# Routing weights of the second expert layer: one-hot matmuls replaced by accumulating indirect DMAs into a cleared matrix

## The chip, the cores and the metric

The kernel runs on one core of one Trainium2 chip. The metric is the device time of one launch in microseconds (us), the median of the timed runs. All arithmetic is float32; a matrix product is done as three products of a high and a low part.

## The reference, cut to what matters

The program is a two-layer block (attention and convolution, an expert layer; a recurrent mLSTM mixer, a second expert layer) followed by a second two-layer transformer. The change is in the second expert layer, and a part of it lies in the mLSTM stage before. An expert layer does this for each token `t` (256 tokens in the second layer, D = 1024, 8 heads, 128 keys per side, so 16384 experts, 16 chosen per head):

```
q = (xb @ w_q).reshape(PEER_BLOCK, PEER_HEADS, 2, PEER_DHALF)
s = jnp.einsum('thpd,hpkd->thpk', q, subkeys).astype(jnp.float32)
s1, i1 = lax.top_k(s[:, :, 0], PEER_TOPK)
s2, i2 = lax.top_k(s[:, :, 1], PEER_TOPK)
cand = s1[..., :, None] + s2[..., None, :]          # 16 x 16 pairs
cidx = i1[..., :, None] * PEER_NKEYS + i2[..., None, :]
top, pos = lax.top_k(cand, PEER_TOPK)
idx = jnp.take_along_axis(cidx, pos, axis=-1)
g = jax.nn.softmax(top, axis=-1)
act = jax.nn.gelu(jnp.einsum('td,thkd->thk', xb, u[idx]))
return jnp.einsum('thk,thkd->td', g * act, v[idx])
```

## The kernel before

The kernel does not gather the chosen experts of the second layer. It computes all 16384 activations for all 256 tokens, multiplies them by a routing matrix that is zero where an expert was not chosen, and multiplies the result by all of v. The expert number is i * 128 + j, with i the first and j the second index of the pair; the routing matrix has one value for each j, i and token.

The function is `experts` (line 964). All engines walk the same slots. The up phase has 144 slots: in each, a piece of 128 x 1024 weights (16 pieces of w_q, 128 of u, one for each j) is loaded by SP into `w_raw` (ring of 3), split into a high part by ScalarE (line 168) and a low part by VectorE (line 173), and multiplied by TensorE in 24 matmuls of 256 columns (`project`). The result of a u piece goes through Gelu on ScalarE and is stored to memory (`spilled`, line 1136). The down phase has 128 slots over v: SP loads the piece and reads the stored activations of 128 experts again (line 1156), VectorE multiplies them by the routing values (`weigh`, line 1535), they are split, and TensorE adds 12 products of 512 columns to four banks (`combine`).

The queries come in four passes of two heads. In the slots after a pass VectorE ranks its scores (`rank_step`, 15 steps spread over 18 slots) and leaves the indices i and j in `sel[:, t, 0]` and `sel[:, t, 1]`. After the last pass only, `centre` (slot 78), an Exp on ScalarE (slot 79) and `normalise` (slot 80) make the softmax weights of all heads, in `sel[:, t, 2]`. Then `turn` (slot 81) transposes the three lists, so that the picks of a token lie along the partitions, and for 64 groups of four tokens (`route`, slots 84 to 135) VectorE and ScalarE build a one-hot matrix of i and one of j that carries the weights, TensorE multiplies them (line 1225: 4 matmuls of 128 x 128, 8 records in the trace), ScalarE copies the result (line 1311), and SP stores it in chunks of 16 tokens of 1 MB (line 1140). When all chunks are stored (waits at line 1144) SP reads the matrix back, 8 values of j at a time (line 1149), into a ring of two.

The order within an engine is the order of the slots in its loop: SP's loads, stores and reads of all these kinds stand in one queue. In the second layer POOL has only the root of the norm. In the first layer, which shares this function, POOL also issues 256 indirect gathers of expert rows for one tile of tokens (line 1167). That layer keeps its way of routing.

The stage before the second expert layer is `mlstm` (line 1808). It loads 33 weight pieces of 512 KB on SP through a ring of three (`Pieces.sp_load`, line 1781), which waits for the split of the piece three before.

Of the kernel before, what the change touches and what calls it, by code (L numbers as in the profile page):

```python
# [17 lines left out]
P = 128  # L18
# [945 lines left out]
def experts(nc, ident, consts, w_q, subkeys, u, v, xs, tiles, gate_rows, spans, spilled, routed_dram, sparse_from):  # L964
# [13 lines left out]
    u_rows, gathered = sparse_from or (None, ())  # L978
    GATHERED = NT - 1 if sparse_from else None
# [6 lines left out]
    pairs_done = {1: 0, 3: 1} if NT > TT else {3: 0}  # L986
# [15 lines left out]
    NG = N // 4  # L1002
# [25 lines left out]
    NC = N // GT  # L1028
    chunk_last = [route_at[4 * k + 3] for k in range(NC)]
    read_from = chunk_last[-1] + (6 if GATHERED is not None else 3)  # L1030

    with Stage(nc) as st:
# [31 lines left out]
        G = arena.at(0, "routing_chunk", [P, 2, NC, JC, GT])  # L1064
# [12 lines left out]
        else:  # L1077
# [21 lines left out]
             "routing_staged", "weighed_ready", "weighed_high_ready", "weighed_split", "sum_kept"))  # L1099
        block = st.begin()  # L1100
# [14 lines left out]

        def bank(n, t):
            return (side if n == 0 else hidden)[:, t, :] if NT == 4 else side[:, 2 * n + t, :]

        @block.sync
        def _(sp):  # L1120
# [3 lines left out]
            sp.dma_start(keys[:, :, :], subkeys).then_inc(keys_loaded, 16)  # L1124
            for s in range(-AHEAD, SLOTS):
# [19 lines left out]
                for k in range(PE_K // JC):  # L1145
                    if s == (read_from + k if k < 2 else UP + JC * (k - 1) - 1):
                        if k >= 2:
                            sp.wait_ge(weighed_ready, JC * (k - 1))
                        sp.dma_start(G[:, k % 2], routed_dram[:, :, k * JC * GT:(k + 1) * JC * GT]
# [9 lines left out]
        def _(pool):  # L1159
            normed.pool_root(pool)  # L1160
            for n, (kind, k) in enumerate(items):
                if n == 0:
                    pool.wait_ge(chosen, 1)
                if n >= GR:
# [4 lines left out]
                    .then_inc(gathered[n % GR], 16)  # L1169

        @block.tensor
        def _(pe):
# [56 lines left out]
            def combine(d):  # L1229
                s = UP + d  # L1230
                pe.wait_ge(weighed_split, d + 1)
                for n in range(2):
                    pe.wait_ge(split, 2 * s + n + 1)
                    if d == 0:
                        pe.wait_ge(staged_in, NG)
                        pe.wait_ge(evacuated, UP)
# [8 lines left out]
            for s in range(UP):  # L1245
# [4 lines left out]
                if s == turn_at:  # L1250
                    turn()
# [7 lines left out]
        def _(act):  # L1259
# [79 lines left out]
            for s in range(SLOTS):  # L1339
# [6 lines left out]
                if s - 1 in finish:  # L1346
                    act.wait_ge(centred, finish[s - 1] + 1)
                    pair = tiles_of(finish[s - 1])
                    nc.scalar.activation(ex[:, pair], top[:, pair].rearrange("p t (h k) -> p t h k", k=K), ACT.Exp) \
                        .then_inc(exp_done, 1)  # L1350
# [4 lines left out]
                if s == turn_at + 1:  # L1355
                    keep_picks()
# [13 lines left out]
        def _(dve):  # L1370
# [96 lines left out]
            def centre(event):  # L1467
                pair = tiles_of(event)
                chain.settle()
                chain.wrote(nc.vector.tensor_copy(total[:, pair], tops[:, pair, :, 0]))  # L1470
                chain.settle()
                nc.vector.tensor_tensor(tops[:, pair], tops[:, pair],
                                        total[:, pair].unsqueeze(3).broadcast_to([P, TT, H, K]), ALU.subtract) \
                    .then_inc(centred, 1)

            def normalise(event):
                pair = tiles_of(event)
                dve.wait_ge(exp_done, event + 1)
                chain.wrote(nc.vector.tensor_reduce(total[:, pair], ex[:, pair], X, ALU.add))
                chain.settle()  # L1480
                chain.wrote(nc.vector.reciprocal(total[:, pair], total[:, pair]))
                chain.settle()
                for t in range(pair.start, pair.stop):
                    last = nc.vector.tensor_tensor(sel[:, t, 2, :].rearrange("p (h k) -> p h k", h=H), ex[:, t],
                                                   total[:, t].unsqueeze(2).broadcast_to([P, H, K]), ALU.mult)
# [42 lines left out]
            def weigh(d):  # L1528
# [4 lines left out]
                if d >= 2:  # L1533
                    dve.wait_ge(weighed_split, d - 1)
                nc.vector.tensor_tensor(weighed[:, d % 2, :].rearrange("p (c t) -> p c t", t=GT),  # L1535
# [272 lines left out]
def mlstm(nc, ident, consts, cols, norm, gate_row, w, xs):  # L1808
# [21 lines left out]
    with Stage(nc) as st:  # L1830
# [31 lines left out]
        half = st.sbuf("minus_half", [P, 2])  # L1862
        acc = [st.psum(f"acc{r}", [P, 512]) for r in range(4)]
# [22 lines left out]
        def _(sp):  # L1886
# [14 lines left out]
        def _(pool):  # L1901
            normed.pool_root(pool)
# [1467 lines left out]
```

## Time and profile before

| | us |
|---|---|
| median of three timed runs | 4600.79 (4597.6 to 4608.13) |
| profiled execution | 4594.13 |
| its span, first to last instruction | 4592.4 |
| TensorE matmul busy | 4179.2 (91%) |
| VectorE busy | 3223.5 (70%) |
| ScalarE busy | 2216.7 (48%) |
| POOL busy | 322.4 (7%) |

The mean granted TensorE clock of the profiled execution was 0.955 of full speed. All other times below are counted from the start of its span. The mLSTM stage runs from 1842 to 2056 us, the second expert layer from 2060 to 2945. Busy time of TensorE is modelled from pipelined matmuls: consecutive records overlap, so a duration of 0.28 us does not mean that a matmul costs 0.28 us; the distance of two starts does. PE is TensorE, PEld its weight load, DVE VectorE, ACT ScalarE, POOL GpSimd, SP the queue engine.

### The profile page before, as it was taken

Reading aid. Unit: us, or ns where it says so; the run is one execution under the profiler, and the core shown is the slowest. Engines: PE = TensorE matmul, PEld = TensorE weight load, DVE = VectorE, ACT = ScalarE, POOL = GpSimd, SP = SyncE. Lnnn points to the kernel's source line nnn. Section 1 sums busy time; section 2 is a strip of 40 time slices with the busy share of each in tenths; the row PEclk is TensorE's granted clock in tenths of the full one; section 3 lists DMA queues with packets and bytes.
Section 4 is the critical chain, followed back from the end, with each engine's and each line's share of the span. In section 5 each row is a group of like instructions: output and inputs, shape, how many; then the busy total and the mean of one; then the engine's idle time right before and its main releaser. Section 6 shows DMA issues by size and latency. Waiting matters only on the chain. (4 is left out here: it accounts for less than half of the span.)

```text
span 4592.4 us, 70641 instructions
## 1 busy us (share of the span) xinstructions
PE 4179.2 (91%) x25113; PEld 3660.3 (80%) x25113; DVE 3223.5 (70%) x7301; ACT 2216.7 (48%) x4317; POOL 322.4 (7%) x301
## 2 busy tenths in 40 slices
PE   7869899999999999889999999699888999988898
PEld 2445799999977777669999777598876889887687
DVE  7636599999878787558877576665486556548655
ACT  6514344367633333335478455444355444435543
POOL 0000002422322221000000000000000000000000
PEclk9889899999999999899999999899999999999899
DMA  8611358888999997227777888554444445444343
GB/s 303 214 40 37 97 166 281 292 277 307 341 360 341 339 335 256 87 88 213 213 232 248 267 261 262 173 185 155 131 134 137 174 165 185 158 126 130 132 176 140
DMA packets 398128, 936.24 MB, mean 204 GB/s; under 512 B 35736, under 2 KB 210072, under 8 KB 381188
## 3 DMA queue, kind: packets, MB, share of 16 engines
q1 hardware_dynamic: 360968, 798.21, 52.4%
q0 software_dynamic: 36864, 134.23, 8.4%
q8 instruction: 167, 2.74, 0.2%
q14 instruction: 129, 1.06, 0.1%
HBM read 838.89 MB, written 93.42 MB: 203 GB/s over the span
## 5 line engine op out<-in xcount | busy, mean ns | idle before, releaser
L173 DVE TENSOR_TENSOR w_low__7<-w_raw__2,w_high__7 128x512 fp32r<-128x512 f32 x544 | 362.3, 688 | 119.6 <-ACT w_high__7 L168 104.8
L173 DVE TENSOR_TENSOR w_low__6<-w_raw,w_high__6 128x512 fp32r<-128x512 f32 x576 | 381.3, 686 | 68.8 <-ACT w_high__6 L168 66.1
L161 PE MATMUL hidden<-hT_high__2,w_high__6 128*128 128x384 f32 (+1 forms) x1280 | 423.5, 331 | 6.5 <-DVE w_low__6 L173 6.5
L162 PE MATMUL hidden<-hT_low__2,w_high__6 128*128 128x384 f32 (+1 forms) x1280 | 419.5, 328 | 0.0
L163 PE MATMUL hidden<-hT_high__2,w_low__6 128*128 128x384 f32 (+1 forms) x1280 | 419.0, 327 | 0.0
L168 ACT ACTIVATE w_high__6<-w_raw 128x512 fp32r<-128x512 f32 x576 | 339.9, 625 | 160.0 <-PE side L163 66.7
L168 ACT ACTIVATE w_high__7<-w_raw__2 128x512 fp32r<-128x512 f32 x544 | 322.0, 624 | 71.3 <-PE side__2 L163 35.7
L161 PE MATMUL hidden__3<-hT_high__4,w_high__7 128*128 128x256 f32 x1152 | 333.4, 289 | 0.0
L162 PE MATMUL hidden__3<-hT_low__4,w_high__7 128*128 128x256 f32 x1152 | 328.7, 285 | 0.0
L163 PE MATMUL hidden__3<-hT_high__4,w_low__7 128*128 128x256 f32 x1152 | 328.2, 285 | 0.0
L161 PEld LDWEIGHTS hidden<-hT_high__2,w_high__6 128*128 128x128 f32 x1280 | 242.3, 189 | 7.8 <-issue 7.2
L163 PEld LDWEIGHTS hidden<-hT_high__2,w_low__6 128*128 128x128 f32 x1280 | 242.5, 189 | 0.0
L162 PEld LDWEIGHTS hidden<-hT_low__2,w_high__6 128*128 128x128 f32 x1280 | 242.3, 189 | 0.0
L161 PE MATMUL side__2<-w_high__7,weighed_high__2_23558 128*128 128x512 f32 x512 | 205.7, 402 | 23.4 <-DVE weighed_low__2_23559 L173 15.3
L161 PEld LDWEIGHTS hidden__3<-hT_high__4,w_high__7 128*128 128x128 f32 x1152 | 220.4, 191 | 0.0
L162 PEld LDWEIGHTS hidden__3<-hT_low__4,w_high__7 128*128 128x128 f32 x1152 | 220.1, 191 | 0.0
L163 PEld LDWEIGHTS hidden__3<-hT_high__4,w_low__7 128*128 128x128 f32 x1152 | 220.1, 191 | 0.0
L162 PE MATMUL side__2<-w_low__7,weighed_high__2_23558 128*128 128x512 f32 x512 | 203.5, 397 | 0.0
L163 PE MATMUL side__2<-w_high__7,weighed_low__2_23559 128*128 128x512 f32 x512 | 203.4, 397 | 0.0
L1167 POOL DMA_INDIRECT gathered_rows<-in_peer_v,chosen_experts x128 | 163.9, 1281 | 418.2 <-DVE gathered_sum L1512 374.8
L168 ACT ACTIVATE weighed_high<-weighed 128x384 fp32r<-128x384 f32 x128 | 67.2, 525 | 247.7 <-DVE weighed L1535 160.7
L1167 POOL DMA_INDIRECT gathered_rows<-in_u_rows,chosen_experts x128 | 140.4, 1097 | 569.8 <-DVE dots L1499 344.8
(980 smaller groups left out, 12523.1 us busy)
## 6 DMA issues: line engine op xcount, KB each, us to landing
w_raw<-in_peer_u SPq DMA_DIRECT2D x128, 512.0 KB
w_raw<-in_peer_v SPq DMA_DIRECT2D x128, 512.0 KB
w_raw__2<-in_peer_u SPq DMA_DIRECT2D x128, 512.0 KB, 4.3
w_raw__2<-in_peer_v SPq DMA_DIRECT2D x128, 512.0 KB, 4.9
w_ring<-in_w_mod SPq DMA_DIRECT2D x96, 256.0 KB, 4.3
w_ring__2<-in_w_mod SPq DMA_DIRECT2D x96, 256.0 KB, 4.4
activated_dram<-activated SPq DMA_DIRECT2D x128, 192.0 KB
routing_dram<-routing SPq DMA_DIRECT2D x24, 1024.0 KB, 10.0
```

What stands on the lines that cost most here:

```text
L161: nc.tensor.matmul(out, lhs[0], rhs[0], start=start, stop=False, skip_group_check=True)
L162: nc.tensor.matmul(out, lhs[0], rhs[1], start=False, stop=False, skip_group_check=True)
L163: return nc.tensor.matmul(out, lhs[1], rhs[0], start=False, stop=stop, skip_group_check=True)
L168: return nc.scalar.activation(high, src, ACT.Copy)
L173: return nc.vector.tensor_tensor(low, src, high.bitcast(F32), ALU.subtract)
L1167: pool.indirect_dma_start(ring[:, n % GR, :], None, rows, bass.IndirectOffsetOnAxis(ap=chosen_at[:, k:k + 1], axis=0)) \
```

## The change

The routing matrix of the second layer gets the layout [j, i, token] in memory. It is set to zero in the mLSTM stage, by 32 DMAs of 512 KB from a tile of zeros that POOL fills; SP issues two of them after each of the piece loads 3 to 18, and waits for all of them at the end of its queue. In the expert layer `centre`, the Exp and `normalise` are done after each of the four passes, for its two heads. `normalise` also computes the address of each pick, (j * 128 + i) * 256 + token, and for each of the 16 picks of a head and each of the two tiles POOL issues an indirect DMA that adds 128 values of 4 bytes (one per token) to the matrix: 256 DMAs in all. A head's DMAs wait for those of the head before it in the same tile. SP waits for all of them in slot 140 and then reads the matrix, 8 values of j at a time, in contiguous runs of 256 tokens. The transposes of the picks, the one-hots, their matmuls, the evacuations and the stores of the routing chunks are gone in this layer. The arithmetic of the first layer is unchanged; its small instructions are issued per tile.

```diff
+    SCATTER = GATHERED is None
-    pairs_done = {1: 0, 3: 1} if NT > TT else {3: 0}
+    pairs_done = {1: 0, 3: 1} if NT > TT else {p: p for p in range(4)}
-    NG = N // 4
+    NG = 0 if SCATTER else N // 4
-    read_from = chunk_last[-1] + (6 if GATHERED is not None else 3)
+    read_from = UP - 4 if SCATTER else chunk_last[-1] + 6
...
 @@ SP
+                        if SCATTER:
+                            if k == 0:
+                                for t in range(NT):
+                                    for r in range(2):
+                                        sp.wait_ge(scattered[t][r], 16 * K * H // 2)
+                            sp.dma_start(G[:, k % 2], routed_dram[k * JC:(k + 1) * JC].rearrange("j i t -> i j t")) \
+                                .then_inc(G_loaded[k % 2], 16)
+                            continue
...
 @@ POOL
+            for p in range(4 if SCATTER else 0):
+                pool.wait_ge(selected, p + 1)
+                for h in range(p * HP, (p + 1) * HP):
+                    for t in range(NT):
+                        if h >= 1:
+                            pool.wait_ge(scattered[t][(h - 1) % 2], 16 * K * ((h - 1) // 2 + 1))
+                        for k in range(h * K, (h + 1) * K):
+                            pool.indirect_dma_start(routed_dram.rearrange("j i t -> (j i t)").unsqueeze(1),
+                                                    bass.IndirectOffsetOnAxis(ap=cell_at[:, t, k:k + 1], axis=0),
+                                                    sel[:, t, 2, k:k + 1], None, compute_op=ALU.add) \
+                                .then_inc(scattered[t][h % 2], 16)
...
 @@ VectorE, normalise
+                if SCATTER:
+                    part = slice(some.start * K, some.stop * K)
+                    dve.wait_ge(token_loaded, 16)
+                    for t in range(NT):
+                        last = nc.vector.scalar_tensor_tensor(flat_at[:, t, part], sel[:, t, 1, part], float(PE_K),
+                                                              sel[:, t, 0, part], ALU.mult, ALU.add)
+                    chain.wrote(last)
+                    chain.settle()
+                    for t in range(NT):
+                        last = nc.vector.tensor_scalar(cell_at[:, t, part], flat_at[:, t, part], float(N),
+                                                       token[:, t:t + 1], ALU.mult, ALU.add)
+                    chain.wrote(last)
...
 @@ mlstm, SP and POOL
+            sp.wait_ge(zeroed, 1)
             for n in range(3, len(sources)):
                 pieces.sp_load(sp, n)
+                if n < 3 + PE_K // 8:
+                    for j in (8 * (n - 3), 8 * (n - 3) + 4):
+                        sp.dma_start(cleared[j:j + 4].rearrange("j i t -> i j t"),
+                                     zeros[:, :].rearrange("p (j t) -> p j t", t=T)).then_inc(cleared_rows, 16)
+            sp.wait_ge(cleared_rows, 16 * PE_K // 4)
...
+            nc.gpsimd.memset(zeros[:, :], 0.0).then_inc(zeroed, 1)
```

## Rows read from the trace of the kernel before

**Rows 1.** Busy time by stretch: us, each engine's busy (records), clock, DMA share, GB/s.

```profile
2086.00:2320.00 234.00, 234.00 (x1958) 234.00 (x1957) 200.91 (x654) 121.67 (x253) 0.00 (x0) 1.00 0.76 215
2320.00:2530.00 210.00, 210.00 (x1791) 210.00 (x1790) 163.62 (x427) 173.26 (x352) 0.00 (x0) 1.00 0.76 244
2565.00:2935.00 370.00, 354.73 (x1499) 282.93 (x1498) 260.51 (x498) 192.13 (x372) 0.00 (x0) 0.99 0.84 258
```

**Rows 2.** Waits in the second expert layer: us, times, longest, for TensorE and SP.

```profile
PE side__2 L161 <- DVE weighed_low__2_23559 L173: 15.3, 14, 3.0
...
SPq L1144 <- DMA routing_dram<-routing__2_23555: 7.1, 1, 7.1
```

**Rows 3.** Timeline of TensorE, first matmul of the down phase: start, us, idle before.

```profile
2560.96 0.76 PE L161 MATMUL side__2<-w_high__7,weighed_high__2_23558 128*128 128x512 f32 x1 [8.10 <-ACT activated__2 L1278]
```

**Rows 4.** Timeline of TensorE around one routing group, up phase.

```profile
2441.44 1.05 PE L1225 MATMUL side__2<-weight_at_j__2_23553,one_hot_i__2_23552 128*128 128x128 f32 x8
...
2442.45 0.29 PE L162 MATMUL hidden__3<-hT_low__4,w_high__7 128*128 128x256 f32 x1
2442.57 0.28 PE L163 MATMUL hidden__3<-hT_high__4,w_low__7 128*128 128x256 f32 x1
...
2445.20 1.05 PE L1225 MATMUL side__2<-weight_at_j__2_23553,one_hot_i__2_23552 128*128 128x128 f32 x8
```

**Rows 5.** Groups by line, second expert layer: count, busy us, mean ns, idle before.

```profile
L173 DVE TENSOR_TENSOR w_low__7<-w_raw__2,w_high__7 128x512 fp32r<-128x512 f32 x544 | 362.3, 688 | 119.6 <-ACT w_high__7 L168 104.8
...
L1225 PE MATMUL side__2<-weight_at_j__2_23553,one_hot_i__2_23552 128*128 128x128 f32 x512 | 65.5, 275 | 0.0
```

**Rows 6.** DMA issues: count, KB each, median us from issue to landing.

```profile
routing_chunk__2_23556<-routing_dram SPq DMA_DIRECT2D x16, 1024.0 KB, 8.0
...
piece_raw<-in_qk SPq DMA_DIRECT2D x8, 512.0 KB, 3.6
```

**Rows 7.** Timeline of VectorE: centring and normalising, slots 78 and 80.

```profile
2307.79 0.42 DVE L1472 TENSOR_TENSOR top__2<-top__2,total__2 128x256 f32<-128x256 f32 x1
...
2314.93 0.41 DVE L1479 TENSOR_REDUCE total__2<-ex__2 128x16 f32<-128x256 f32 x1
...
2315.67 0.49 DVE L1484 TENSOR_TENSOR selected__3<-ex__2,total__2 128x128 f32<-128x128 f32 x2
```

**Rows 8.** Timeline of ScalarE, slot 79.

```profile
2308.72 1.28 ACT L1349 ACT_TABLE_LOAD   x1
```

**Rows 9.** Timelines of SP and POOL in the mLSTM stage.

```profile
1847.14 1.04 POOL L208 TENSOR_TENSOR inv__4<-mean__4,root__4 128x4 f32<-128x4 f32 x1 [0.47 <-DVE mean__4 L214]
...
1860.63 28.65 SPq L1781 DMA_DIRECT2D piece_raw<-in_qk  x6
1891.55 38.66 SPq L1781 DMA_DIRECT2D piece_raw<-in_v  x8
```

**Rows 10.** Busy time by stretch: mLSTM stage, and first expert layer.

```profile
1892.00:1932.00 40.00, 40.00 (x172) 32.96 (x171) 9.24 (x14) 10.72 (x19) 0.00 (x0) 0.96 0.34 98
...
1300.00:1500.00 200.00, 195.81 (x850) 158.79 (x849) 164.78 (x266) 78.71 (x146) 47.90 (x48) 1.00 0.98 343
```

**Rows 11.** Timeline of POOL, first gathers of the first expert layer.

```profile
719.66 1.32 POOL L1167 DMA_INDIRECT gathered_rows<-in_u_rows,chosen_experts  x1 [216.45 <-DVE chosen_experts L1489]
...
722.88 0.94 POOL L1167 DMA_INDIRECT gathered_rows<-in_u_rows,chosen_experts  x1 [0.30 <-issue]
...
728.45 0.94 POOL L1167 DMA_INDIRECT gathered_rows<-in_u_rows,chosen_experts  x1 [0.30 <-issue]
```

**Rows 12.** The gathers by tile: duration ns min/median/max, first and last start.

```profile
L1167 POOL DMA_INDIRECT gathered_rows<-in_u_rows,chosen_experts x128: 932/1008/1743, 719.7 to 1722.8; - x128
...
L1167 POOL DMA_INDIRECT gathered_rows<-in_peer_v,chosen_experts x128: 932/1007/2886, 770.5 to 1794.5; - x128
```

**Rows 13.** DMA queues: packets, MB, share of 16 engines' span.

```profile
q1 hardware_dynamic: 360968, 798.21, 52.4%
q0 software_dynamic: 36864, 134.23, 8.4%
```

More of the change, by code:

```diff
@@ L977, in experts @@
     NT = len(tiles)
-    u_rows, gathered = sparse_from or (None, ())
-    GATHERED = NT - 1 if sparse_from else None
+    u_rows, gathered = sparse_from
+    GATHERED = NT - 1 if u_rows is not None else None
     ND = NT if GATHERED is None else NT - 1
@@ L1099, in experts @@
              "routing_staged", "weighed_ready", "weighed_high_ready", "weighed_split", "sum_kept"))
+        token_loaded = st.sem("token_numbers_loaded")
+        scattered = [gathered[2 * t:2 * t + 2] for t in range(NT)]
         block = st.begin()
@@ L1249, in _ @@
                         score(p)
-                if s == turn_at:
+                if s == turn_at and not SCATTER:
                     turn()
@@ L1347, in _ @@
                     act.wait_ge(centred, finish[s - 1] + 1)
-                    pair = tiles_of(finish[s - 1])
-                    nc.scalar.activation(ex[:, pair], top[:, pair].rearrange("p t (h k) -> p t h k", k=K), ACT.Exp) \
-                        .then_inc(exp_done, 1)
+                    pair, some = tiles_of(finish[s - 1]), heads_of(finish[s - 1])
+                    for t in range(pair.start, pair.stop):
+                        last = nc.scalar.activation(ex[:, t, some], top[:, t].rearrange("p (h k) -> p h k", k=K)[:, some],
+                                                    ACT.Exp)
+                    last.then_inc(exp_done, 1)
                 if s in gelu_at:
@@ L1354, in _ @@
                     nc.scalar.activation(gelled[:, batch], dots[:, batch], ACT.Gelu).then_inc(gelu_done, 1)
-                if s == turn_at + 1:
+                if s == turn_at + 1 and not SCATTER:
                     keep_picks()
@@ L1482, in normalise @@
                 chain.settle()
                 for t in range(pair.start, pair.stop):
-                    last = nc.vector.tensor_tensor(sel[:, t, 2, :].rearrange("p (h k) -> p h k", h=H), ex[:, t],
-                                                   total[:, t].unsqueeze(2).broadcast_to([P, H, K]), ALU.mult)
+                    last = nc.vector.tensor_copy(total[:, t, some], tops[:, t, some, 0])
+                chain.wrote(last)
+                chain.settle()
+                for t in range(pair.start, pair.stop):
+                    last = nc.vector.tensor_tensor(
+                        tops[:, t, some], tops[:, t, some],
+                        total[:, t, some].unsqueeze(2).broadcast_to([P, some.stop - some.start, K]), ALU.subtract)
@@ L3226, in build @@
         first["gathered"] = [ctx.enter_context(nc.semaphore(f"rows_gathered{r}")) for r in range(GATHER_RING)]
+        first["scattered"] = [ctx.enter_context(nc.semaphore(f"weights_scattered{r}")) for r in range(2 * TT)]
         first_block(nc, ident, consts, cols, first, xs, mod_rows, spilled, routed)
```

68 lines of the change are left out of this document (45 added, 23 removed).

## The prediction

> **What bounds the kernel now.** I read the page first (TensorE busy for 91% of the span), then the table of busy time by stretch, the groups of instructions, the timelines of single engines, and the waits. The changed code is the second expert layer. It consists of an up phase (144 slots: 16 query pieces, 128 pieces of u) and a down phase (128 slots over v). In [rows 1] the reader is to see that TensorE is busy for every one of the 234 us before the routing and of the 210 us with it, at clock 1.00, while VectorE has 33 and 46 us to spare and ScalarE more. So there what TensorE issues sets the time, and work taken from VectorE or ScalarE alone buys nothing. In the down phase TensorE is busy 355 of 370 us, and its only wait of size is the one for the low part of the weighed activations, 15.3 us in 14 times [rows 2]. Between the phases it stands still for 8.10 us [rows 3].
>
> **What goes.** A plain up slot is 24 matmuls, which start 0.12 us apart (2442.45, 2442.57): 2.88 us. From one routing group's start to the next (2441.44 to 2445.20) it is 3.76 us [rows 4]. A group costs TensorE 0.88 us, there are 64, one in each of 52 slots or a second in a slot: 64 x 0.88 = 56.3 us. The six transposes of the picks go too; at the spacing of the eight records of one group (512 records in 64 [rows 5]: 0.88 / 8 = 0.11 us) they are 0.7 us. Together 57.0 us, all on the path, as TensorE never waits there. The one-hots on VectorE and the 64 evacuations on ScalarE go as well and count nothing: both engines lie beside TensorE. Next late in the freed stretch is TensorE itself at 2.88 us a slot: VectorE needs two splits of 0.69 us for it [rows 5].
>
> **The end of the up phase.** SP waits 7.1 us at line 1144 until the last stored routing chunks have landed, with the loads of v behind it [rows 2]; TensorE's 8.10 us follow from this [rows 3]. The changed kernel stores no chunks, and if the scatters are through by slot 140 the wait is nothing. Left is the read of the first chunk, 8.0 us [rows 6], issued three slots (8.6 us) before its use. I leave 2 us of the gap and count 6 us gained (bounds: 0 and 8.1).
>
> **The down phase.** A chunk of 1 MB was read in runs of 16 tokens by 8 j, 512 bytes; now they are 1 KB. The 14 waits for the low part (15.3 us in all [rows 2]) are one for each chunk read from k = 2 on. The bounds are 0 and 15.3; half the runs might halve the DMA's surplus, not the bytes, and I take a third, 5 us. The multiply of 128x256 keeps its size.
>
> **What is added on VectorE and ScalarE.** Centring and normalising now come after each of the four passes, over two heads and two tiles. The present ones take 0.42 us for the subtraction, 0.41 for the sum, 0.25 for each multiply [rows 7]. Fourteen small instructions a pass, at 0.17 to 0.29 us, are some 3.5 us; three passes more are 10 us out of 33 idle [rows 1]. The low part for slot s + 3 is made in slot s, so a pass may be late by two slots (5.8 us) before TensorE sees it. ScalarE gets three more Exp, each with two table loads of 1.28 us [rows 8], out of 112 us idle. I count 0.5 us for both, with the token load (bounds 0 and 5); without this cover it would be 10 + 8 us.
>
> **The clearing, in the recurrent stage before.** 32 DMAs of 512 KB follow piece loads 3 to 18 on SP's queue. SP first waits for POOL's fill of the zeros: POOL is through with its root at 1848.2, and SP's fourth load leaves only at 1860.63 [rows 9], so 12 us cover the fill. Pieces leave every (38.66 - 0.33) / 7 = 5.48 us. Three times the bytes in that time is 1.57 MB / 5.48 us = 287 GB/s; the stretch had 98 GB/s [rows 10]. Traffic with many 1 KB runs has moved at 258 GB/s at share 0.84 [rows 1], and long rows at 343 [rows 10]. At 343 it fits; at 258 each piece is 0.6 us late, 16 pieces 10 us, against a load that lands in 3.6 us [rows 6] and is wanted two pieces (11 us) later. Bounds 0 and 20 us (the upper one if writes in 1 KB runs go slower than any row shows); I take 2, since the two rows near 287 fall either side.
>
> **The scatters.** 256 indirect DMAs of 128 elements on POOL, each adding 4 bytes. Nothing else is on POOL in the stage, but SP waits for all of them at slot 140, and behind it in SP's queue stand the first two routing chunks, the loads of v from slot 147 on, the last stored activations and the first ones read again: TensorE needs all of these. So the date of the last scatter decides this change.
> - Start: the weights were done at 2316.2 [rows 7], in slot 80. The first pass is now done in slot 26, 54 slots earlier: 54 x 2.88 = 155.5, and three blocks of scores of 16 such records as in the routing, 3 x 16 x 0.11 = 5.3. That gives 2155.4.
> - Date: TensorE ended the up phase at 2560.96 - 8.10 = 2552.9 [rows 3], now 57.0 earlier: 2495.9. Less a chunk's landing (8.0) and a scatter's landing (no row; I take a piece's 3.6 [rows 6]): the last one must leave at 2484.3.
> - 328.9 us for 256: the allowance is 1.285 us each. Passes come 54 us apart and bring 64 each, 82 us of work, so POOL doesn't run dry.
> - Price: the trace has indirect gathers of 128 rows of 4 KB, none that scatters or adds. Their instruction is 0.93 us at least, 1.01 in the median, with 0.30 between two: 1.24 or 1.31 [rows 11, 12]. Seven back to back, beside a full VectorE, leave every (728.45 - 719.66) / 6 = 1.465 us [rows 11]. Below: 1.24. Above: an accumulation may want twice the work of writing it down, 2 x 1.01 + 0.30 = 2.3 us. I take 1.31, the median: one entry for each of 128 partitions is what a scatter has too, and VectorE is less full here than beside those seven. 256 x 1.31 = 335.4, so SP and TensorE are late by 6.5 us.
> - The waits of head h for head h - 1 of the same tile stand 16 issues (21 us) behind: nothing.
>
> **Sum.** -57.0 - 6 + 6.5 - 5 + 0.5 + 2 = -59.0 us. The profiled execution took 4594.13 us (span 4592.4 and 1.7 around it); that gives 4535.1. The median of the timed runs, 4600.79, lies 6.7 above it, so I forecast 4542 for such a median. Its own range, with intervals of 1.24 to 1.45 and the bounds above, is 4522 to 4580. Every 0.01 us on a scatter's interval beyond 1.285 costs 2.6 us; the gain without stall is 65.5 us, so the change breaks even at 1.285 + 65.5 / 256 = 1.54 us.
>
> **Rivals.**
> - **A. An adding scatter costs POOL more than a gather (ends slower).** Each element is read at its source and at its target and then written: three accesses to write down for two. With the 1.01 us growing by half, the interval is 1.01 x 1.5 + 0.30 = 1.81; the last leaves at 2155.4 + 463.4 = 2618.8, 134.5 us late instead of 6.5: 4594.1 - 65.5 + 134.5 = 4663 in the profiled execution, 4670 as a median. It decides from 1.54 us on. For it: the shortest gather was 932 ns with either source [rows 12], and POOL went on before the rows had landed, so the time goes into writing the transfer down, not into moving it. Against: a fixed part of it may be large. Chance 0.24. On its premise the Trainium skill, "DMA: Bandwidth & Descriptors", section "Rules for kernel authors", says that an accumulating DMA reads its destination and writes it later; no row here shows what this costs.
> - **B. The DMA engines can't take the small packets (ends slower).** SP's queue moves 640 KB per 2.88 us, 228 GB/s of the 350 that 343 at share 0.98 means [rows 10]: 65%. A gather made 36864 / 256 = 144 packets, 9 an engine; scatters would be 2304 an engine. At the mean of SP's queue, 0.524 x 4592.4 x 16 / 360968 = 107 ns [rows 13], they are 246 us; with 214 of the rest this is 460 us of work in 329: +131 us, so 4594 - 65.5 + 131 = 4660, 4666 as a median. At 50 ns they just fit. The 107 ns are for 2.2 KB, which speaks against it; that each adds in memory speaks for it. Chance 0.12.
> - **C. VectorE holds POOL up.** The first gather, which began beside VectorE's splits, took 1.32 us, the third 0.94 [rows 11]. Splits fill 2 x 0.69 of 2.88 us, less their overlap some 42%: 0.94 + 0.42 x 0.38 + 0.30 = 1.40 us. 256 x 1.40 = 358.4: 29.5 us late, 23 above the forecast: 4565 as a median. Chance 0.14. The Trainium skill, "SBUF — State Buffer", section "Who interferes with whom", has this as a rule: a VectorE instruction with two inputs in SBUF contends with a GpSimd instruction that reads SBUF; the trace agrees by the 1.32 against 0.94 us.
> - **D. The clearing starves the piece loads**: 20 us instead of 2, 4559. Chance 0.04.
> - **E. The gain is eaten to nothing**: an interval of 1.50 to 1.58. 4590 to 4611. Chance 0.05.
>
> **Chances and range.** Forecast 0.41, C 0.14, D 0.04: 0.59, all faster. A and B 0.36, slower, though the mildest of A may be near the break-even. E 0.05. A measurement here can tell 0.2% (9 us) from no change. Faster 0.60, same 0.04, slower 0.36. Both signs hold much chance, so the range must reach over A and B: 4522 to 4675; above it is POOL's upper bound of 2.3 us (+125 us more than A).
>
> **What would show it.** In the changed profile: no matmul at line 1225 in the second layer and up slots of 2.88 us to the end (if they are longer and ScalarE waits for loads of w_raw, B); 256 DMA_INDIRECT on POOL from about 2155 on, whose interval is 1.31 (C: 1.40 with long ones beside splits; A: 1.5 or more throughout); SP's wait for scattered at slot 140 as the one before the first matmul of the down phase, under 8 us by the forecast, over 100 by A; pieces 5.5 us apart in the recurrent stage. The forecast is wrong if that last wait is above 30 us.

## The result, and the profile after

| | before | after |
|---|---|---|
| median of the timed runs, us | 4599.19 (4 runs) | 4708.93 (4 runs) |
| profiled execution's span, us | 4592.4 | 4694.2 |
| up phase, first matmul to end, us | 481.3 | 418.2 |
| gap before the down phase, us | 8.1 | 179.4 |
| down phase, first to last matmul, us | 379.8 | 373.5 |

The kernel got slower: ratio 1.0232, 95% interval 1.0210 to 1.0254. The forecast was 4542, with 0.6 on faster. The time is rival A's case and beyond it: 4709 where A gave 4670.

The page of the changed kernel first: TensorE's busy time, the two large DMA queues, and the new group of instructions (busy us, mean ns, idle before).

```profile
PE 4115.7 (88%) x24595; PEld 3593.7 (77%) x24595; DVE 3134.8 (67%) x7039; ACT 2128.0 (45%) x4137; POOL 747.8 (16%) x558
...
q1 hardware_dynamic: 359320, 798.22, 51.2%
q0 software_dynamic: 73728, 134.38, 10.0%
...
L1199 POOL DMA_INDIRECT routing_dram<-selected__3,routing_cells x256 | 423.1, 1653 | 172.8 <-DVE selected__3 L1539 95.0
```

TensorE is busy for 63.5 us less than before, as meant, and the time is longer all the same: busy time that goes is not time won. The table by stretch shows where it went. Its stretches are the up phase, the gap and the down phase; they answer to [rows 1].

```profile
2077.00:2495.00 418.00, 418.00 (x3522) 418.00 (x3520) 293.57 (x843) 225.15 (x461) 280.86 (x164) 0.99 0.89 222
2495.00:2674.60 179.60, 0.27 (x3) 0.06 (x1) 1.71 (x4) 1.31 (x4) 142.27 (x93) 0.51 0.25 13
2674.60:3049.00 374.40, 364.98 (x1536) 290.44 (x1536) 264.91 (x507) 194.31 (x377) 0.00 (x0) 0.99 0.81 261
```

The reader is to see the middle row. For 180 us every engine but POOL stands still, and the DMA engines are at share 0.25. POOL is the only one at work, and the 142 us that it is busy in 180 are one instruction after another with 0.3 us between them. The waits say for whom (these answer to [rows 2]; us, times, longest):

```profile
PE side__2 L161 <- ACT activated__2 L1311: 179.4, 1, 179.4
PE side__2 L161 <- DVE weighed_low__2_23605 L173: 9.2, 10, 2.0
...
SPq L1167 <- DMA routing_dram<-selected__3,routing_cells: 179.8, 2, 150.3
```

The first row names ScalarE's last activation, which had long been done: it is the last semaphore in the list of the waiting matmul. The third row has the true one: SP at line 1167 waits for the scatters, with the first chunks and the loads of v behind it. The scatters began like this (timeline of POOL):

```profile
2164.43 1.83 POOL L1199 DMA_INDIRECT routing_dram<-selected__3,routing_cells  x1 [95.00 <-DVE selected__3 L1539]
2166.56 1.56 POOL L1199 DMA_INDIRECT routing_dram<-selected__3,routing_cells  x1 [0.30 <-issue]
2168.42 1.55 POOL L1199 DMA_INDIRECT routing_dram<-selected__3,routing_cells  x1 [0.30 <-issue]
2170.28 6.22 POOL L1199 DMA_INDIRECT routing_dram<-selected__3,routing_cells  x1 [0.31 <-issue]
2176.80 1.61 POOL L1199 DMA_INDIRECT routing_dram<-selected__3,routing_cells  x1 [0.30 <-issue]
```

The last one left at 2663.79, so the interval is 499.36 / 255 = 1.958 us, where I had 1.31 and a break-even of 1.54. Nothing in the price is waiting for an earlier one: the idle time between two is "issue", 0.30 us, throughout. Three instructions took over 6 us. That is what VectorE did in the same time as the first of them:

```profile
2170.13 2.48 DVE L173 TENSOR_TENSOR w_low__7<-w_raw__2,w_high__7 128x512 fp32r<-128x512 f32 x4
2172.53 0.22 DVE L1458 CAST where_f__2<-where__2 128x128 bf16<-128x128 uint32 x1
2172.66 1.22 DVE L1459 TENSOR_TENSOR pair_scores__2_23594<-best__2 128x1024 f32<-128x1024 f32 x1
2173.80 1.29 DVE L173 TENSOR_TENSOR w_low__7<-w_raw__2,w_high__7 128x512 fp32r<-128x512 f32 x2
2175.01 0.42 DVE L1423 MAX8 head_top__2<-pair_scores__2_23594 128x8 f32<-128x256 f32 x1
```

The long scatter starts inside an unbroken run of subtractions, cast and addition, and ends at 2176.50, which is 1.49 us after the start of the MAX8 that closes the run.

### The profile page after: what moved, and what is told of

Read it like the earlier page. It is cut to its first block and busy times, and to the rows that moved or that the text cites. A ratio compares the mean times of both kernels' runs of the same rounds, so it can differ in the third digit from the quotient of the medians.

```text
span 4694.2 us, 69369 instructions
## 1 busy us (share of the span) xinstructions
PE 4115.7 (88%) x24595; PEld 3593.7 (77%) x24595; DVE 3134.8 (67%) x7039; ACT 2128.0 (45%) x4137; POOL 747.8 (16%) x558
## 5 line engine op out<-in xcount | busy, mean ns | idle before, releaser
L1199 POOL DMA_INDIRECT routing_dram<-selected__3,routing_cells x256 | 423.1, 1653 | 172.8 <-DVE selected__3 L1539 95.0
L162 PE MATMUL hidden<-hT_low__2,w_high__6 128*128 128x384 f32 (+1 forms) x1280 | 418.4, 327 | 0.0
L161 PE MATMUL side__2<-w_high__7,weighed_high__2_23604 128*128 128x512 f32 x512 | 205.3, 401 | 188.7 <-ACT activated__2 L1311 179.4
L161 PE MATMUL hidden__3<-hT_high__4,w_high__7 128*128 128x256 f32 x1152 | 324.7, 282 | 0.0
L162 PE MATMUL hidden__3<-hT_low__4,w_high__7 128*128 128x256 f32 x1152 | 324.2, 281 | 0.0
L163 PE MATMUL hidden__3<-hT_high__4,w_low__7 128*128 128x256 f32 x1152 | 324.2, 281 | 0.0
L161 PEld LDWEIGHTS side__2<-w_high__7,weighed_high__2_23604 128*128 128x128 f32 x512 | 97.2, 190 | 217.3 <-DVE weighed_low__2_23605 L173 195.0
L161 PEld LDWEIGHTS hidden__3<-hT_high__4,w_high__7 128*128 128x128 f32 x1152 | 218.2, 189 | 0.0
L162 PEld LDWEIGHTS hidden__3<-hT_low__4,w_high__7 128*128 128x128 f32 x1152 | 218.1, 189 | 0.0
L163 PEld LDWEIGHTS hidden__3<-hT_high__4,w_low__7 128*128 128x128 f32 x1152 | 218.1, 189 | 0.0
L1592 DVE TENSOR_TENSOR weighed__2_23603<-activated_again__2_23606,routing_chunk__2_23602 128x256 f32<-128x256 f32 x128 | 53.9, 421 | 234.7 <-DMA activated_again__2_23606<-activated_dram 234.1
```

Of the source, the lines that this page charges most:

```text
L161: nc.tensor.matmul(out, lhs[0], rhs[0], start=start, stop=False, skip_group_check=True)
L162: nc.tensor.matmul(out, lhs[0], rhs[1], start=False, stop=False, skip_group_check=True)
L163: return nc.tensor.matmul(out, lhs[1], rhs[0], start=False, stop=stop, skip_group_check=True)
L1199: pool.indirect_dma_start(routed_dram.rearrange("j i t -> (j i t)").unsqueeze(1), bass.IndirectOffsetOnAxis(ap=cell_at[:, t, k:k + 1], axi ...
L1592: nc.vector.tensor_tensor(weighed[:, d % 2, :], act_in[:, d % AD, :], G[:, k % 2, d % JC, :], ALU.mult) \
```

## The experiments

The recurrent stage began at 1846.6 and 1860.2 us in the two profiles of the code of before, and between 1845.2 and 1856.7 us in the eight of the changed code, whose first layer differs only in how small instructions are issued. So single times are read to about 10 us, and the stages of the second layer are compared by their own lengths.

### Is it the adding, the scatter, or the number of cells?

Plain writes in place of adding ones (e1_plain):

```diff
-                                sel[:, t, 2, k:k + 1], None, compute_op=ALU.add)
+                                sel[:, t, 2, k:k + 1], None)
```

> The scatters write instead of adding (left out: the sum where two heads of a token chose the same expert). Everything else as in the changed kernel. Theory 1, the adding is what makes a scatter dear on POOL: the instruction falls from 1.54 us (median) to the 0.93 to 1.01 us of the gathers of the first layer, the interval from 1.96 to about 1.31 us, the last scatter of 256 issues near 2164 + 335 = 2499, and the gap of TensorE before the down phase falls from 179 us to about 20; time about 4709 - 160 = 4550. Theory 2, it is scattering itself, adding or not: instruction 1.54 us, interval 1.96 us, gap 179 us, time 4709. Theory 3, adding costs at the DMA engines alone (a read and a write at each cell) and POOL is held back by them: the landing, 2.9 us in the changed kernel, falls, and the interval with it, but not to 1.31.

The same cells gathered into a buffer (e3_gather4):

```diff
-    pool.indirect_dma_start(cells_of(routed_dram), IndirectOffsetOnAxis(ap=cell_at[:, t, k:k + 1], axis=0),
-                            sel[:, t, 2, k:k + 1], None, compute_op=ALU.add)
+    pool.indirect_dma_start(fetched[:, t, k:k + 1], None, cells_of(routed_dram),
+                            IndirectOffsetOnAxis(ap=cell_at[:, t, k:k + 1], axis=0))
```

> Each of the 256 scatters is turned round into a gather of the same 128 cells of 4 bytes, from the routing matrix into a column of a buffer in SBUF (left out: the routing weights never reach the matrix). Theory 1, direction decides (an instruction that scatters costs 1.54 us, one that gathers 0.93 to 1.01, whatever its size): interval about 1.31 us, gap about 20 us, time about 4550. Theory 2, the form of the list decides (128 separate cells of 4 bytes, in place of 128 rows of 4 KB): 1.54 us, interval 1.96 us, gap near 179 us, time 4709.

Adding scatters over 64 partitions (e4_64):

```diff
-    IndirectOffsetOnAxis(ap=cell_at[:, t, k:k + 1], axis=0), sel[:, t, 2, k:k + 1], None, compute_op=ALU.add
+    IndirectOffsetOnAxis(ap=cell_at[0:64, t, k:k + 1], axis=0), sel[0:64, t, 2, k:k + 1], None, compute_op=ALU.add
```

> Each of the 256 adding scatters takes partitions 0 to 63 alone, 64 cells in place of 128 (left out: the weights of the other half of the tokens). Theory 1, POOL pays for each cell: of 1.54 us half goes, interval 1.96 - 0.77 = about 1.2 us, the last scatter issues before 2484, gap below 10 us, time about 4535. Theory 2, POOL pays for the instruction: interval stays between 1.8 and 1.96 us, gap 140 to 179 us, time 4670 to 4709. In between, the two intervals at 64 and 128 cells give a fixed part and a part for each cell.

Measured, one run each: 4578.21, 4577.65 and 4689.22 us. TensorE's gap before the down phase is 50.0, 46.6 and 161.4 us, the interval of the instructions 1.456, 1.442 and 1.890 us. The instruction by tile (duration ns min/median/max, first and last start us), for the plain scatter:

```profile
L1199 POOL DMA_INDIRECT routing_dram<-selected__3,routing_cells x256: 954/959/5405, 2165.7 to 2537.0; - x128
```

for the gather:

```profile
L1200 POOL DMA_INDIRECT fetched_cells<-routing_dram,routing_cells x256: 940/946/5432, 2171.1 to 2538.9; - x128
```

and for the adding scatter over 64 partitions:

```profile
L1199 POOL DMA_INDIRECT routing_dram<-selected__3,routing_cells x256: 1421/1427/4949, 2172.9 to 2654.8; - x128
```

A plain scatter costs POOL 0.96 us and a gather of the same cells 0.95, close to the 0.93 of the shortest gather of 4 KB rows [rows 12]: neither direction nor size matters much to it. Adding makes it 1.54: 0.58 us more. Half the cells save 0.12 of 1.54 us, some 1.8 ns a cell: of the 1.54 us about 0.23 go with the number of cells and 1.31 are fixed. A plain scatter of 64 cells was not run, so at least 0.35 of the adding's 0.58 us are a price for the instruction, and how the rest divides is not shown. Of the first two, theory 1 was right about the instruction; of the third, theory 2. Theory 3 of the plain scatters (POOL held back by the DMA engines) does not fit: in both kernels POOL idles 0.30 us between two, and what shrank is the instruction itself. From the last scatter's start to the first down matmul it is 10.9 us with adding and 10.0 without.

But theory 1's time for the first two, 4550, was missed by 28 us, and that is a second finding. Their interval is not 1.31 us, though the median instruction is shorter than the 1.01 that I had assumed. The plain kernel's timeline of POOL shows why, once beside VectorE's subtractions and once in the gap, when VectorE had stopped (e1_plain):

```profile
2398.56 1.28 POOL L1199 DMA_INDIRECT routing_dram<-selected__3,routing_cells  x1 [0.30 <-issue]
2400.14 0.96 POOL L1199 DMA_INDIRECT routing_dram<-selected__3,routing_cells  x1 [0.30 <-issue]
2401.41 1.28 POOL L1199 DMA_INDIRECT routing_dram<-selected__3,routing_cells  x1 [0.30 <-issue]
2402.99 0.96 POOL L1199 DMA_INDIRECT routing_dram<-selected__3,routing_cells  x1 [0.30 <-issue]
...
2535.76 0.96 POOL L1199 DMA_INDIRECT routing_dram<-selected__3,routing_cells  x1 [0.30 <-issue]
2537.03 0.96 POOL L1199 DMA_INDIRECT routing_dram<-selected__3,routing_cells  x1 [0.30 <-issue]
```

And VectorE in the same kernel and time:

```profile
2401.16 1.29 DVE L173 TENSOR_TENSOR w_low__7<-w_raw__2,w_high__7 128x512 fp32r<-128x512 f32 x2 [1.56 <-ACT w_high__7 L168]
2404.01 1.29 DVE L173 TENSOR_TENSOR w_low__7<-w_raw__2,w_high__7 128x512 fp32r<-128x512 f32 x2 [1.55 <-ACT w_high__7 L168]
```

Here a scatter that starts inside a pair of subtractions is 0.32 us longer; the ones between pairs, and all of them after VectorE has stopped, take 0.96. Over 256 the mean is 1.150 against a shortest of 0.954: VectorE costs 0.196 us a scatter, 50 us in all. Counted over the whole kernel, 110 of the 256 start beside a subtraction or an addition of the pair scores, and they hold 46.9 of these 50 us. In the changed kernel it is 66 of 256, which hold 26.3 of 28.2 us above 1.542 us each. Even without adding, the scatters come too late: the gap of this kernel is 50.0 us.

### Does VectorE hold the scatter?

Two breaks in VectorE's run (e8_break):

```diff
                 elif k == 5:
+                    nc.vector.max(breaks[:, p, 0, :], iota)
                     nc.vector.tensor_copy(where_f[:, :, :, :], where[:, :, :, :])
-                    chain.wrote(nc.vector.tensor_tensor(cand[...], best[...], best[...], ALU.add))
+                    nc.vector.tensor_tensor(cand[...], best[...], best[...], ALU.add)
+                    chain.wrote(nc.vector.max(breaks[:, p, 1, :], iota))
```

> The changed kernel with two MAX8 of a constant row (0.3 us each, results unused) put into VectorE's step that makes the pair scores: one ahead of the cast to bf16, one behind the addition. In the changed kernel three scatters took 6.2 to 6.3 us, each from the start of an unbroken run of VectorE's subtractions, cast and addition until the MAX8 behind it began, plus 1.54. Theory 1, such a run holds POOL's scatter off and MAX8 lets it through: the first MAX8 comes 2.5 us after the run's start, so the three long ones shrink to 3.9 to 4.2 us. Theory 2, they are something periodic of POOL's own or of its queue: they stay at 6.2 to 6.3 us. The span changes by less than 10 us either way.

Measured: 4711.54 us (one run). Timeline of POOL beside the second of the three runs:

```profile
2229.89 3.86 POOL L1200 DMA_INDIRECT routing_dram<-selected__3,routing_cells  x1 [0.30 <-issue]
2234.06 2.56 POOL L1200 DMA_INDIRECT routing_dram<-selected__3,routing_cells  x1 [0.30 <-issue]
```

Timeline of VectorE there:

```profile
2229.86 2.48 DVE L173 TENSOR_TENSOR w_low__7<-w_raw__2,w_high__7 128x512 fp32r<-128x512 f32 x4
2232.26 0.28 DVE L1459 MAX8 breaks__2<-iota 128x8 f32<-128x128 f32 x1
...
2233.93 1.27 DVE L173 TENSOR_TENSOR w_low__7<-w_raw__2,w_high__7 128x512 fp32r<-128x512 f32 x2
2235.13 0.42 DVE L1424 MAX8 head_top__2<-pair_scores__2_23602 128x8 f32<-128x256 f32 x1
```

The 6.3 us are 3.86 now (3.74 and 3.86 at the other two): the scatter is through 1.49 us after the MAX8 that was put in. The next one starts in the following pair of subtractions, and again ends 1.49 us after the start of the MAX8 behind that pair (2236.62 and 2235.13). Theory 1 held. TENSOR_TENSOR alone does this, as the run of four shows; MAX8 lets the scatter through. This agrees with the Trainium skill, "SBUF — State Buffer", section "Who interferes with whom", by which a VectorE instruction with two SBUF inputs blocks a GpSimd one that reads SBUF. The same section infers that writing down a transfer is not hit by tensor_tensor; for an indirect DMA the 3.86 against 1.54 us say otherwise.

But the hold does not always last to the end of a run. In the plain kernel's pair above, the second subtraction started at 2401.77, and the scatter was through 0.91 us later, at 2402.69: it got in between the two. In the changed kernel, of 48 scatters that start inside the first of such a pair, 36 end 1.50 us after the start of the second subtraction and only 5 follow the whole pair. What decides between the two is not shown.

### Do the other terms of the sum hold?

Only the scatters of heads 0 to 3, so that nothing is late (e2_half):

```diff
-            for p in range(4 if SCATTER else 0):
+            for p in range(2 if SCATTER else 0):
...
-                                        sp.wait_ge(scattered[t][r], 16 * K * H // 2)
+                                        sp.wait_ge(scattered[t][r], 16 * K * H // 4)
```

> Only the 128 scatters of heads 0 to 3 are issued (left out: the routing weights of heads 4 to 7); the clearing, the additions on VectorE and ScalarE and the reads of the chunks stay. Theory 1, the whole loss is the wait for the last scatter, and the other terms of my sum hold: the first down matmul no longer waits (gap 1 to 3 us, of 179.4), the up phase stays at 418 us, the down phase at 374 us, time 4709 - 177 = 4532 us, ratio to the kernel before 0.985. Rival, the scatters also slow what runs beside them (VectorE held off SBUF, DMA engines busy with small packets): with half of them gone the up phase becomes shorter than 418 us by 3 us or more and a down phase without queued scatters too, time below 4528. Rival, once the wait is gone another one takes its place before the first chunk read or the first weighed block (a landing of 7.8 us behind the last up piece): gap of 8 us or more, time above 4538.

Measured in 3 rounds: 4537.71 us (4525.20 to 4540.92), ratio 0.9862, interval 0.9846 to 0.9879. Its up and down phases by stretch:

```profile
2071.00:2489.00 418.00, 417.78 (x3517) 417.61 (x3516) 293.34 (x842) 225.37 (x460) 228.20 (x128) 1.00 0.88 226
2491.00:2880.00 389.00, 365.30 (x1534) 291.13 (x1535) 264.67 (x506) 194.65 (x378) 0.00 (x0) 0.99 0.78 251
```

TensorE's waits in the down phase:

```profile
PE side__2 L161 <- DVE weighed_low__2_23605 L173: 23.5, 14, 3.0
PE side__2 L161 <- ACT activated__2 L1311: 1.4, 1, 1.4
```

The gap is 1.4 us and the up phase the same 418 us (418.4) with half as many scatters beside it, so the scatters take nothing from TensorE. Theory 1 held for the time. The down phase did not: 388.6 us, 9 longer than before. Over the ten profiles of this document:

| kernel | gap, us | down phase, us | its waits for the low part, us |
|---|---|---|---|
| before | 8.1 | 379.8 | 15.3 |
| before, buffers moved (below) | 8.7 | 386.1 | 18.2 |
| half the scatters | 1.4 | 388.6 | 23.5 |
| clearing twice (below) | 0.6 | 383.0 | 19.6 |
| one tile of two (below) | 3.2 | 386.6 | 21.0 |
| gather | 46.6 | 383.4 | 18.5 |
| plain | 50.0 | 380.5 | 14.5 |
| 64 partitions | 161.4 | 378.1 | 14.5 |
| two breaks | 177.0 | 379.8 | 15.6 |
| changed kernel | 179.4 | 373.5 | 9.2 |

The difference of the last two columns is 363 to 368 us each time: the waits, not the matmuls, make the length, and 1 KB runs in place of 512 bytes are not shown to lower them. The two kernels with the routing of before lie 6.3 us apart, and the one with the breaks has the changed kernel's pause and the length of before:

```profile
L161 PE MATMUL side__2<-w_high__7,weighed_high__2_23612 x512: 390/393/767, 2679.1 to 3058.9; 128*128 128x512 f32 x171
```

So the 6.3 us that the changed kernel gained here are no more than the spread between profiles. Pauses of 46 us and more go with somewhat shorter down phases, but the two groups overlap, and no run tried a pause by itself.

The clearing done twice, on top of this kernel (e7_clear2):

```diff
                         sp.dma_start(cleared[j:j + 4]..., zeros...).then_inc(cleared_rows, 16)
+                        sp.dma_start(cleared_too[j:j + 4]..., zeros...).then_inc(cleared_rows, 16)
```

> As the kernel with the scatters of heads 0 to 3 alone, and the clearing done twice (a second matrix of 16.8 MB is cleared beside the first and not used). Theory 1, the clearing is hidden (it cost 1.1 us of the mLSTM stage in the changed kernel): from the mLSTM stage's start to the first up matmul 226 to 229 us, and no other stage moves. Theory 2, the loads of the pieces were near their limit and the second 16.8 MB starve them: 16.8 MB at the 343 GB/s that the trace of before shows elsewhere are 49 us beside 33 MB of pieces in the same 36 us, so the stage grows by 30 us or more.

Measured: 4542.24 us (one run). From the stage's start (fill of its root) to the first up matmul it is 225.0 us before (225.2 with moved buffers), 226.2 after, 225.6 with half the scatters and 236.8 here: the second 16.8 MB cost 11 us, the first about 1.1 (0.5 to 2.6 over the kernels that clear the whole matrix once). Neither theory had the 11 us. Busy time in the stretch of the clearing in the changed kernel (last two columns: DMA share and GB/s; before they were 0.34 and 98 [rows 10]):

```profile
1892.00:1932.00 40.00, 37.51 (x174) 31.08 (x174) 12.66 (x22) 11.31 (x21) 0.00 (x0) 1.00 0.98 320
```

and with the clearing done twice:

```profile
1905.00:1985.00 80.00, 68.48 (x289) 55.35 (x288) 20.41 (x50) 20.41 (x44) 3.06 (x8) 0.94 1.06 363
```

One clearing fills the DMA engines to 0.98 and just fits; the next one is late.

### What the up phase gained beyond 57 us

The up phase fell by 62.9 us (first to last matmul 480.7 to 417.8), not 57. Its matmuls came every 0.119 us in place of 0.120. The kernel before, with nothing changed but three unused buffers set aside in the second expert layer (e6_moved):

```diff
+        if sparse_from is None:
+            st.sbuf("flat_experts", [P, NT, H * K])
+            st.sbuf("routing_cells", [P, NT, H * K], U32)
+            st.sbuf("token_numbers", [P, TT])
```

> The kernel before with three small unused buffers (2 x 1 KB and 8 bytes in each partition) set aside where the changed kernel has its cell numbers, so that all later buffers of the second expert layer lie at the changed kernel's places. Theory 1, the up phase's matmuls of 256 columns come every 0.119 us in place of 0.120 in the changed kernel because their buffers lie elsewhere: here too the median matmul is 281 to 282 ns (287 before) and the up phase is 3 to 5 us shorter than 481 us. Theory 2, it has to do with what was taken out (one-hots) or the shape of the program: 287 ns and 481 us stay.

The high x high matmuls of the up phase by tile, in the kernel before (duration ns min/median/max, first and last start):

```profile
L161 PE MATMUL hidden__3<-hT_high__4,w_high__7 x1152: 274/287/562, 2071.6 to 2552.3; 128*128 128x256 f32 x192
```

and in this one:

```profile
L161 PE MATMUL hidden__3<-hT_high__4,w_high__7 x1152: 277/280/562, 2085.4 to 2559.7; 128*128 128x256 f32 x192
```

474.3 us in place of 480.7: 6.4 us come from where the buffers lie, and 62.9 - 6.4 = 56.5 are the routing's, against 57.0 forecast. That is from one profile each; the up phases of the six other kernels without one-hots are 418.4 to 420.1 us, so 54 to 56.5 is what can be said. Theory 1 held, if a little stronger than expected. Its time, 4606.81 us, is one run and shows no gain: in the same profile the down phase is 6.3 us longer than before. Which address does it stays open.

### A version that beats both

The adding scatters are worth having as far as they fit before slot 140. So the first tile of 128 tokens is scattered (128 instructions) and the second keeps its one-hots (32 groups); the cleared matrix is half as large (e5_hybrid). This version computes everything.

```diff
-    NG = 0 if SCATTER else N // 4
+    HOT = (1,) if SCATTER else tuple(range(ND))
+    NG = len(HOT) * P // 4
...
+            G0 = arena.at(0, "routing_cells_chunk", [P, 2, JC, P])
+            G = arena.at(8 * KB, "routing_chunk", [P, 2, NC, JC, GT])
...
-                    for t in range(NT):
+                    for t in range(1):
                         if h >= 1:
                             pool.wait_ge(scattered[t][(h - 1) % 2], 16 * K * ((h - 1) // 2 + 1))
...
+                    nc.vector.tensor_tensor(weighed[:, d % 2, 0:P], act_in[:, d % AD, 0:P], G0[:, k % 2, d % JC, :], ALU.mult)
```

> A version that computes everything: the first tile of 128 tokens gets its routing weights by 128 adding scatters into a cleared matrix of 128 x 128 x 128, the second tile by 32 groups of one-hot matmuls as before. Theory 1, the interval of 1.96 us and the landing waits between heads hold for half as many scatters: 128 x 1.96 + 8 x 3 = 275 us from 2164, so the last lands near 2440, ahead of the first chunk read near 2515, and nothing waits for it. The up phase gives back 32 x 0.88 + 0.35 = 28.5 of its 63 us: 447 us; gap 1 to 3 us; down phase 380 to 389 us (with one tile less time no pause lets the loads run ahead). Time about 4600 - 34.5 - 6.5 + 4 = 4563 us, ratio 0.992. Rival, two reads for each chunk and two multiplications for each block make the down phase longer by over 6 us: 4570 or more, ratio 0.994 to 1.0. Rival, routing groups on TensorE are slower beside scatters (both want VectorE's time): up phase 455 us or more.

Measured in 5 rounds: 4568.76 us (4564.93 to 4581.86), ratio 0.9945 to the kernel before, interval 0.9928 to 0.9962, so 0.4 to 0.7% faster, where 4563 us and 0.992 were expected. Its up and down phases by stretch:

```profile
2076.00:2522.00 446.00, 445.65 (x3781) 445.48 (x3779) 338.36 (x995) 275.92 (x560) 228.95 (x128) 1.00 0.86 231
2525.50:2912.00 386.50, 365.46 (x1533) 290.68 (x1534) 270.73 (x633) 194.30 (x377) 0.00 (x0) 0.99 0.83 252
```

Its scatters by tile, and what POOL waited for (us, times):

```profile
L1202 POOL DMA_INDIRECT routing_cells_dram<-selected__3,routing_cells x128: 1541/1556/6221, 2163.7 to 2453.9; - x128
...
  DMA routing_cells_dram<-selected__3,routing_cells: 26.2, 7
```

Its first down matmul:

```profile
2525.46 0.47 PE L161 MATMUL side__2<-w_high__7,weighed_high__2_23589 128*128 128x512 f32 x1 [3.25 <-ACT activated__2 L1314]
```

The last scatter leaves 61 us before the first chunk is read (2515.0), in spite of seven waits between heads of 26.2 us in all. The up phase is 445.7 us, 35.0 shorter: 6.4 by place and 28.6 for 32 groups, as expected (28.5). The down phase took 386.6 us, 6.8 longer than before, which is at the bound of the rival there; as the kernel before took 386.1 us in its other profile, the two multiplications are not shown to cost anything.

## Why the prediction was wrong, step by step

- **What bounds the kernel, and the routing (-57.0).** Right: 54 to 56.5 by the runs. Another 6.4 came from moved buffers, which I had not thought of.
- **The end of the up phase (-6).** Right where it can be seen: 1.4 us of the 8.1 are left with half the scatters, -6.7.
- **The down phase (-5).** Its size was met by luck (-6.3 in the changed kernel's profile), and its reason is not borne out. The seven kernels with 1 KB runs and whole chunks took 373.5 to 388.6 us, the two of before 379.8 and 386.1; the size of the runs in memory is not shown to give anything.
- **VectorE, ScalarE (+0.5) and the clearing (+2).** Right: the up phase has no wait from them; the clearing cost 1.1, and rival D's 20 us did not come. "At 343 it fits" was the true side, at 320 GB/s.
- **The scatters' start and date.** The first left at 2164.43 where I had 2155.4, of which 5.4 are the second expert layer's later begin; TensorE ended the up phase at 2495.2 where I had 2495.9, as that later begin and the gain from the moved buffers cancel.
- **The step that failed: "I take 1.31, the median".** Measured it is 1.958 = 0.955 for a plain scatter + 0.588 for adding + 0.110 for VectorE + 0.305 us of POOL's idle time between two. By my own rule of 2.56 us for each 0.01 us, (1.958 - 1.285) x 256 = 172 us of lateness: 4594.1 - 65.5 + 172.3 = 4701 in the profiled execution, 4708 as a median, against 4708.93. For the plain scatters it gives 4594.1 - 65.5 + 43.8 = 4572 in a profiled execution, or 4579 as a median, against 4578.21 in the one run, which is the profiled one. So the chain from interval to time was sound, and the price of one instruction was nearly the whole error. That the medians agree to 1 us is luck: the changed kernel's profiled execution took 4695.88 us, 5 less than 4701, and its median lies 13 us above that, where I had added 6.7.
- **Rival A was right** in its place and sign: adding costs POOL's instruction 1.6 times a plain one (1.54 to 0.96), where I had 1.5. I gave it 0.24 because every row at hand was a gather; "a fixed part of it may be large" was no reason against it, as most of the price is fixed. Its reason, three accesses for each element in place of two, is not shown, and the run over 64 partitions speaks against it: half the elements saved 0.12 of 1.54 us. It alone gives (0.955 + 0.588 + 0.305) = 1.85 us: (1.85 - 1.285) x 256 = 145, a median of 4680.
- **Rival C was right as well**, and I had held A and C to be alternatives. With plain scatters it is 0.196 us each (1.456, where I wrote 1.40), with adding ones 0.110; 28 us of the loss. The trace of before had it: the seven gathers at 1.465 us beside a full VectorE [rows 11] gave the plain interval to 1% (partly by chance, as the instructions beside them were others), and I chose the median of single instructions in its place. The median also hides the three scatters of over 6 us. That splits fill 42% of VectorE's time is a slip of no weight: a pair takes 1.29 of 2.88 us, which is 45% and 0.01 us more.
- **Rival B was wrong.** With VectorE and all loads at rest the scatters still came every 1.85 us at a DMA share of 0.25, so the engines that move the packets were not what held them.

## What to carry to other kernels

A serial queue of many small instructions is priced by the mean interval beside the engines that will run then, not by the median of one instruction in a quiet stretch; and where the form needed is in no row, as adding was here, the price of a neighbouring form can be far too low (here 0.96 for 1.54 us). Before swapping matmuls for indirect DMAs, divide the time from first index to last use by their number: here 1.285 us, and the instruction costs 1.85 even with nothing beside it. Where all don't fit, a share may: half of them hidden gave 0.55%.

## What the runs showed of the hardware

- An adding indirect DMA over 128 partitions, one cell each, costs POOL 1.54 us, over 64 partitions 1.43, a plain one 0.96, a gather 0.95; 0.30 us lie between two.
- A TENSOR_TENSOR of VectorE with both inputs in SBUF holds such an instruction off. In the changed kernel 36 of 48 scatters got in between the two of a pair, and the three longest only when a run of subtractions, cast and addition ended; the longest hold was 4.8 us. A MAX8 put into the run let the scatter through (6.34 us became 3.86).
- A scatter of 128 cells counts 144 packets, as a gather of 128 rows does: the queue went from 36864 [rows 13] to 73728.
- After the gap TensorE's clock had fallen. The granted clock is 0.51 of full in the gap's row above, and the first matmuls of 512 columns came every 0.43 us, then every 0.23 (timeline, changed kernel):

```profile
2677.76 0.63 PE L162 MATMUL side__2<-w_low__7,weighed_high__2_23604 128*128 128x512 f32 x1
2678.18 0.63 PE L163 MATMUL side__2<-w_high__7,weighed_low__2_23605 128*128 128x512 f32 x1
2678.61 0.55 PE L161 MATMUL side__2<-w_high__7,weighed_high__2_23604 128*128 128x512 f32 x1
2679.00 0.40 PE L162 MATMUL side__2<-w_low__7,weighed_high__2_23604 128*128 128x512 f32 x1
2679.24 0.39 PE L163 MATMUL side__2<-w_high__7,weighed_low__2_23605 128*128 128x512 f32 x1
```

  That is the level of 1.2 GHz and then of 2.4. Ten matmuls at the lower one cost 10 x 0.2 = 2 us after a standstill of 179 us. It does not take a long standstill: the kernel before started its down phase at the lower level too, after 8.1 us, and left it at its eighth matmul:

```profile
2563.65 0.58 PE L161 MATMUL side__2<-w_high__7,weighed_high__2_23558 128*128 128x512 f32 x1
2564.07 0.39 PE L162 MATMUL side__2<-w_low__7,weighed_high__2_23558 128*128 128x512 f32 x1
2564.30 0.40 PE L163 MATMUL side__2<-w_high__7,weighed_low__2_23559 128*128 128x512 f32 x1
```
- The place of buffers in SBUF moved the cadence of 256-column matmuls from 0.120 to about 0.119 us, 6.4 us in this phase (one profile on the old places, nine on moved ones).
